# Setting a stage's semaphores to nought: one instruction for a run of neighbouring numbers in place of one for each semaphore

## What is computed

```python
def reference(x, c, ctx, ...):
    x = first_block(x, c, ctx, ...)
    return second_block(x, ...)

# first_block: modulation from c; input projection of 512 + 256 tokens; short
#   convolution; chunked gated delta rule in two directions; output projection;
#   16 experts, each of which takes its 64 best tokens; RMS norm
# second_block, twice: a mixer (retention with differential attention, then
#   latent attention with gated linear attention), layer norm, 32 experts of
#   which each token takes two, layer norm
```

## Time and profile before

| | us |
|---|---|
| median of three runs (lowest, highest) | 3031.14 (3026.56, 3033.29) |
| profiled execution, whole | 3035.76 |
| its span, first to last instruction | 3034.0 |
| PE busy | 2606.5 |
| DVE busy | 879.1 |
| ACT busy | 623.0 |
| POOL busy | 238.5 |
| mean granted clock of TensorE, share of full speed | 0.93 |

### The profile page before, as it was taken

How to read it: one execution, slowest core, us unless ns; L and a number is a source line. 1 busy time by engine, 2 the same in 40 slices (tenths; PEclk the granted TensorE clock), 3 DMA queues, 4 the chain that set the end, 5 groups by cost and what they waited for, 6 DMA issues and landing times. The chain is left out here.

```text
span 3034.0 us, 42491 instructions
## 1 busy us (share of the span) xinstructions
PE 2606.5 (86%) x17577; PEld 1352.2 (45%) x17577; DVE 879.1 (29%) x1831; ACT 623.0 (21%) x1213; POOL 238.5 (8%) x213
## 2 busy tenths in 40 slices
PE   6997787869999999998889989974998889988983
PEld 3544686433334334445454444432346644434441
DVE  2664573331121121456430000003333651000002
ACT  4412442310001011333111101102223321110112
POOL 0100443100000000001100000001001320000001
PEclk8998898879999999999989999997999889999997
DMA  8231202549999983001569999994303227999996
GB/s 316 84 136 59 72 4 82 192 186 418 417 415 413 399 340 122 22 1 56 188 265 424 429 428 429 428 382 168 105 1 132 76 96 296 429 427 427 427 428 242
DMA packets 109843, 755.43 MB, mean 249 GB/s; under 512 B 20980, under 2 KB 24416, under 8 KB 70768
## 3 DMA queue, kind: packets, MB, share of 16 engines
q1 hardware_dynamic: 106224, 738.38, 59.6%
q0 software_dynamic: 2592, 12.58, 1.1%
q10 hardware_dynamic: 864, 2.10, 0.2%
HBM read 727.07 MB, written 25.97 MB: 248 GB/s over the span
## 5 line engine op out<-in xcount | busy, mean ns | idle before, releaser
L1962 PE MATMUL bank<-ring,expert_in 128*64 128x512 f32 x1536 | 343.5, 602 | 21.8 <-DMA ring<-in_moe_w_up_dram 18.7
L1897 DVE TENSOR_TENSOR hidden<-silu_gate,bank 128x512 f32<-128x512 f32 x32 | 33.7, 1054 | 736.9 <-PE bank L1962 736.9
L1691 PE MATMUL bank<-ring,expert_in 128*64 128x512 f32 x1024 | 224.8, 597 | 8.2 <-DVE home L1539 5.5
L1962 PEld LDWEIGHTS bank<-ring,expert_in 128*64 128x64 f32 x1536 | 121.2, 139 | 238.0 <-issue 235.3
L1973 PE MATMUL bank<-ring,hidden_T 128*64 128x512 f32 x768 | 170.1, 595 | 31.8 <-ACT hidden_T L1921 31.8
L1951 PEld LDWEIGHTS bank<-onehot,x_part 128*128 128x128 bf16 x3072 | 175.3, 99 | 31.4 <-issue 24.3
L1951 PE MATMUL bank<-onehot,x_part 128*128 128x128 bf16 x3072 | 180.8, 221 | 6.8 <-DVE onehot L1888 6.8
L1691 PEld LDWEIGHTS bank<-ring,expert_in 128*64 128x64 f32 x1024 | 73.4, 138 | 157.3 <-issue 141.6
L1706 PE MATMUL bank<-ring,hidden_T 128*64 128x512 f32 x512 | 122.3, 639 | 3.6 <-ACT hidden_T L1614 3.6
L2688 PE MATMUL bank<-ring,home 128*128 128x512 f32 x256 | 118.6, 625 | 6.3 <-PEq L194 6.3
L610 PE MATMUL bank<-home,ring 128*128 128x512 f32 (+1 forms) x320 | 113.9, 515 | 7.6 <-PEq L194 7.6
(11 more groups left out here) (653 smaller groups left out, 3711.8 us busy)
## 6 DMA issues: line engine op xcount, KB each, us to landing
ring<-in_moe_w_gate_dram SPq DMA_DIRECT2D x52, 2048.0 KB, 20.1
ring<-in_moe_w_up_dram SPq DMA_DIRECT2D x50, 2048.0 KB, 24.7
ring<-in_moe_w_down_dram SPq DMA_DIRECT2D x50, 2048.0 KB, 26.6
ring<-in_w_gate_dram SPq DMA_DIRECT2D x32, 2048.0 KB, 13.1
ring<-in_w_up_dram SPq DMA_DIRECT2D x32, 2048.0 KB, 14.5
ring<-in_w_down_dram SPq DMA_DIRECT2D x32, 2048.0 KB, 16.0
ring<-in_w_mod_dram SPq DMA_DIRECT2D x12, 2048.0 KB, 10.3
home<-in_moe_w_down_dram SPq DMA_DIRECT2D x9, 2048.0 KB, 27.7
```

The lines of the kernel that those rows point to most:

```text
L1691: mm = pe.matmul(B[2 + 2 * part + b][rows, :], xe[:, dc, rows], ws[e][:, c, b * COLS:(b + 1) * COLS], start=(dc == 0), stop=(dc == NC - 1))
L1962: mm = pe.matmul(B[2 + 2 * part][rows, :], xe[:, c, rows], ws[e][:, c, :], start=(c == 0), stop=(c == NC - 1))
```

## The change

A helper joins sorted semaphore numbers into runs of neighbours, and SP clears each run with one instruction.

```diff
+def runs_of(numbers):
+
+    runs = []
+    for n in numbers:
+        if runs and runs[-1][1] == n:
+            runs[-1] = (runs[-1][0], n + 1)
+        else:
+            runs.append((n, n + 1))
+    return runs
+
+
 @contextmanager
 def stage(m):
...
         yield sem, m.buffers(ctx)
-        for s in sems:
-            nc.sync.sem_clear(s)
+        for first, end in runs_of(sorted(s.num for s in sems)):
+            nc.sync.sem_clear(range(first, end))
         nc.all_engine_barrier()
```

## The result

| | before | changed |
|---|---|---|
| median, four runs each, us | 3031.58 | 3004.96 |
| lowest to highest | 3026.56 to 3033.29 | 3003.77 to 3011.83 |
| span of the profiled execution | 3034.0 | 3003.5 |
| PE busy | 2606.5 | 2590.0 |
| mean granted clock | 0.93 | 0.94 |

The ratio is 0.9912, with a 95% interval from 0.9898 to 0.9925: 26.6 us faster, between 23 and 31. Two later sessions with the same kernel gave 0.9911 and 0.9913. The time lies inside the range and on the forecast side, but the gain is 5 to 6 us larger than the 21 us of the sum, and so outside the forecast's own 21 give or take 4: the range holds it only because it was drawn to take in rival C. The profiled span fell by 30.5 us; some 4 us of this are owed to the execution profiled before the change, which took 3035.76 us where the median is 3031.58.

The account below looks back on a forecast made before the run. The prediction took all engines' waits for SP's clears at stage ends as what counts. Terms 21.1 + 0.5 - 0.7 = 20.9, rounded to 21 us, off the 3031.1 us median gave 3010 us; range 3003 to 3017.

Parts of the forecast that it names:

- rival C: At 2322 us a shorter pause may keep full clock, 2.3 us; three stretches 7 us, 3003 us; 10 in 100.
- Everybody waits for SP, and the starts count (1): At stage ends, 371 clears removed at 57 ns from start to start, all on every engine's path: 21.1 us gained.
- The irregular row (2): At 2321.8 us, a stall among 29 clears most likely goes: 0.5 us gained, bounds 0 and 0.5.
- The floor (3): At 13 changed ends with one or two clears, SP is no longer last: 0.7 us of gain lost, 0 to 1.3.
- The wide clear (4): A clear over a range up to 49 wide takes the same 57 ns slot as a single one.
- rival B: The wide clear walks its range: at 57 ns a number 3031 us, at 75 ns 3038; 3 in 100 slower, 3 equal.
- Everything behind only shifts (5): Behind the barriers all work moves forward, also in the expert stages, and nothing of the gain is absorbed.
- Rival A: At stage ends the clears cover instruction fetches, so the gain shrinks to nothing, 3031 us; 4 in 100 for full loss.

Follow-up runs that it names:

- the single barrier: Changed kernel without the stage's second barrier; semaphores keep their numbers one stage more and are cleared at the next stage's beginning: 0.9911 and 0.9908 against the kernel before.
- the pieces of two: Changed kernel with each run of neighbours cut into clears of two numbers, 209 clears: 3024.86 us, 0.9972 against the kernel before.

## Why the prediction was right, and where it was short

The cost of the clears was predicted rightly, in mechanism and in size: 20.9 us forecast, 20.35 measured between the releases. The 26.6 us of the whole are that and some 6 us more, which the forecast had at nothing and only rival C named.

*Everybody waits for SP, and the starts count (1).* Right. 371 clears at 57 ns were 21.1 us; the stretches between the releases gave 20.35 us, and the doubled clears cost 57 ns each where a row was regular, 64 on the mean.

*The irregular row (2).* It went: the four clears at that end run from first clear to release in 0.4 us. But a new one came, at the end of the gated linear attention, where the first two of three clears start 0.48 us apart. That end takes 0.89 us from release to release, and 0.43 in the kernel with the twelfth end long, where three clears run regularly. By this term I gained 0.5 us and lost 0.46.

*The floor (3).* Right where one clear is left: 0.3 us from clear to release. What I missed is that the floor isn't the same at every end. At the even mixer's end POOL's DRAIN of 184 ns, long hidden under the clears, now comes last, and the end takes 0.69 us, some 0.26 more than the 0.43 of three regular clears.

*The wide clear (4).* I took one slot whatever the width. By the durations it is 1.7 ns a number dearer, at most 401 x 1.7 ns = 0.7 us in all. Little of that is on the path, because PE's DRAIN, at 509.9, stands just ahead of SP's, at 510.0, even behind the widest clear. From release to release the end with one clear of 49 takes 0.37 us, those with one clear of 12 to 33 take 0.33 to 0.34. What lies between 20.9 and 20.35 is more than covered by the 0.46 and the 0.26 above. The price from which rival B would have decided, 57 ns, is thirty times that. Rival B is excluded.

*Everything behind only shifts (5).* This is the step that failed, in both directions. In the expert stages it held nearly: the two token stages moved by less than 1.1 us, between 486.3 and 488.4. But stages 13 and 10 became shorter by 4.4 to 6.1 and 1.9 to 3.1 us, and the last one longer by 1.3 to 1.9. That the total still fell inside the range is owed to the width of the range and not to this step.

*Rival C, the clock.* It named the place, the low clock behind the pause at 2322 us, and the direction. The 6.8 us of low clock there are gone in the first profile and halved in the two others of the changed kernel, and all four profiles with the long clears at that end have them in full. As a price it was right for no profile: 2.3 us for the one stretch, where the stage became 4.4 to 6.1 us shorter, since it has 14 to 17 us less of low clock in all and the later stretches fall differently too. In the medians the two runs that isolate the twelfth end give it less, 2 to 4 us with the clears' own 1.9. The runs' mean clock says that the 6 us beyond the barriers go with less low clock over the whole program; how they divide among the stages is open. The total of 3003 us that I gave to this rival is nearer to the 3005 measured than the forecast's 3010. Ten in a hundred was too little for something whose rows were on the table.

*Rival A, the code.* The full loss is excluded. Something like it may be there in small: at the last stage the clears covered a load of code, and without them 1.6 us are lost, though by late data and not by an engine without its instructions. The row that I had weighed for it (PE's DRAIN behind the jumped block) is unchanged:

```profile
L2372 POOLq DRAIN  x2: 34/34/34, 2004.1 to 2962.9; - x2
L2372 PEldq DRAIN  x2: 8/34/60, 2064.7 to 2967.4; - x2
```

POOL is ready at 2962.9 and PE at 2967.4, 4.5 us apart where it was 4.4, so that wait is no business of the clears. The Trainium skill (Runtime: NRT & Kernel Launch, section Instruction fetch mechanics) says that a taken branch to a page not at hand stalls. This row is in keeping with that, though no run moved the code to test it. The entries into the stages show no such stall after the change: at each of the fourteen behind which PE has work, its first instruction comes at most 0.1 us later behind the release than it did before, 0.1 us behind it at the even mixer's end in both kernels.

## What to carry to other kernels

Where all engines wait for one, count that engine's small instructions and price them by the distance between their starts; an instruction that is said to take 25 ns can cost 57, and 371 of them were 20 us that no busy share shows. After such a pause is shortened, look at the granted clock on its far side before and after: here some 6 of the 27 us gained lay beyond the barriers, with less low clock in every session, and one stage of the profile shows 4 to 6 us of it behind a shortened pause. And before the last microsecond is taken out of a pause, ask what is loaded during it, code included. One end here hid more than its clears cost, 1.6 us against 1.0, and the single barrier took out 6.7 us between the stages and won nothing by it.

## What the runs showed of the hardware

- A semaphore clear takes 25 to 30 ns for one number and 1.7 ns for each more: 45 ns for 12, 108 ns for 49. From one single clear to the next SP needs 57 ns in a regular row; 401 more clears cost 64 ns each on the mean.
- With 5.1 us or more between two matmuls at the barrier of stage 12 the granted clock fell to 1.2 GHz for 6.8 us behind it, in four profiles of four, and with 4.3 us (the pieces of two) it did the same. With 2.9 to 3.3 us, in the same list of instructions, it stayed at 2.4 GHz there in three profiles and fell for 3.4 us in four.
- An engine's DRAIN at a barrier isn't always short: POOL's took 34 to 47 ns at sixteen ends and 183 to 190 ns at one, and it held the barrier up once nothing else was later.
- Where a load of 16 KB of code began 0.7 us or less before a gather, beside 1 MB of other loads, the gather's rows were used 8.4 to 9.1 us after its issue in six profiles of seven; where it began 1.6 us or more before, 7.2 to 7.3 us in five of five.
- In the two profiles of the kernel before, eleven of the seventeen stages repeat within 0.1 us, and the delta rule's differs by 2.8. In other kernels they repeat less well: the even mixer's stage took 274.3 and 277.3 us in two profiles of the changed kernel, the thirteenth 87.5 and 91.2 in two of the single barrier.
